# Two transformer layers on one core: the second layer's modulation made in the first feed-forward part, and the layer loop written out

## The chip, the core and the metric

The kernel runs on one core of a Trainium2 chip. The core has a matrix engine (TensorE, PE in the profile; PEld are its weight loads), VectorE (DVE), ScalarE (ACT), GpSimd (POOL) and SyncE (SP, here the main DMA queue). They run independently and wait for one another by semaphores. Weights and activations come from the chip's memory (HBM) by DMA into SBUF; PE writes its results to PSUM, eight banks of 512 fp32 columns. The metric is the device time of one execution in microseconds (us); lower is better.

## The reference, cut to what matters

Two layers run on 1024 latent tokens and 128 context tokens (1152 columns together), model width 1024. Each layer has its own modulation: a row of 6 x 1024 numbers from a conditioning vector, one for the context and one for the latents, which shifts, scales and gates both halves of the layer.

```python
for l in range(DEPTH):                                   # DEPTH = 2
    mod_ctx = silu(c_ctx) @ w_ada[l] + b_ada[l]          # w_ada[l]: 1024 x 6144
    mod_lat = silu(c) @ w_ada[l] + b_ada[l]
    ...
def trunk_layer(x, mod, ...):
    shift1, scale1, gate1, shift2, scale2, gate2 = split(mod, 6)
    h = rms_norm(x, g1) * (1 + scale1) + shift1
    x = x + gate1 * token_mixers(h, ...)                 # 6 MLA heads, 6 GQA heads, an FFT mixer, w_out
    h = rms_norm(x, g2) * (1 + scale2) + shift2
    x = x + gate2 * ((silu(h @ w_gate) * (h @ w_up)) @ w_down)   # width 2816
```

The modulation needs only the conditioning vectors and w_ada, so the kernel is free to place it anywhere ahead of its use.

## The kernel before

Everything lies transposed: channels on the 128 partitions, tokens in the columns, in three groups of 384. For precision each fp32 product is made of three matmuls on high and low parts (`mm3`, L1662 to L1666): GpSimd splits each weight unit of 128 x 1024 into w_hi (a cast, L851 and L918) and w_lo (a subtraction, L853 and L920), VectorE and ScalarE split the activations. All waits are written by hand, so the order on each engine is the order of the code.

The engines' programs are a preamble, a loop over the two layers (`Fori(0, DEPTH)`, a loop at run time on every engine; what depends on the layer is a register, and so are the values that its waits compare with), and the final norm. A layer is: norm, input projection, FFT mixer, up-projections; twelve heads, an MLA head and a GQA head in turn, in a function `pair` that runs for p = 0 to 5, the middle ones in a loop; the output projection w_out; the second norm; and the feed-forward part in 11 chunks of 256 hidden channels (a loop). One chunk is six tiles of gate and up (48 matmuls each) and 24 down units of 6 matmuls. VectorE's part of a tile is three operations (L1628 product, L1631 high part, L1633 low part); of a down unit, one or two (`add_gated`, L1606).

The modulation comes in 24 blocks of 512 columns, 12 per layer. Blocks 0 to 3 of layer 0 are made in the preamble by PE (`ada_w`). The others are made beside the heads, one block per head. SP loads the block, 2 MB in four DMAs, into `ada_buf` (`load_ada`, L720), which lies over the weight ring that the heads don't use. VectorE multiplies and adds it up over the eight rows of k, for context and latents (`ada_sums`, L1529, 16 operations of 512 columns, L1540 and L1542), three k ahead of the maxima of the next head, five behind. In the next head PE turns the sums from columns to partitions and adds over the partitions with 8 matmuls against ones (`ada_turn`, L1953, fp32, so 16 passes in the profile), and VectorE adds the bias into `mod` (`ada_add`, L1517, L1525). Which block head (p, w) makes is told by `late_chunk` (L246). In layer 0, heads 0 and 1 make blocks 0 and 1 of layer 1, heads 10 and 11 its blocks 2 and 3, the others layer 0's blocks 4 to 11. In layer 1 the same code makes layer 1's blocks 4 to 11, and heads 0, 1, 10 and 11 make layer 0's blocks 0 to 3 once more. The last head's block has its turn behind the heads (L1992).

Three things stand around this. GpSimd waits for all twelve blocks of the layer (L893) before it splits the first three units of w_out (L895), since the ring lies under `ada_buf` and `ada_acc`. Behind the heads, the heads' outputs come back from memory by `load_mix` (L754), one tile after another in a ring of four; each waits until `mix_low` (L1582, L1585) has made the low part of the tile four before it; PE's first out-projection tile needs eight of them. And SP loads the feed-forward weights (L794 to L804), each into one of three stages, as soon as GpSimd has split what was there.

In the heads PE makes the scores (L1899 to L1902), the products with V (L1917) and, for the next head, scores in full for the row maxima (`max_scores`, L1940), which VectorE reduces from PSUM (L1514); PE waits for each reduction before the next.

Of the kernel before, what the change touches and what calls it, by code (L numbers as in the profile page):

```python
# [245 lines left out]
def late_chunk(p, w, l):  # L246

    if isinstance(p, int) and p in (0, HEADS - 1):
        return l * -1 + 1, (0 if p == 0 else 2) + w
    return l, ADA_PRE + 2 * (p - 1) + w  # L250


def build(nc, a, o):
    ctx = ExitStack()
    with ctx:
# [48 lines left out]
        neg_max = keep("neg_max", [P, 16])  # L304
        y_stat = keep("y_stat", [P, 5, 9])
        ph = at[0]

        def phase(first, *tensors):
# [31 lines left out]
        qst_m, mq_hi, mq_lo, mk_hi, mk_lo, mv, ga, gb, ka, kb, gv, kst_g = phase(  # L340
# [3 lines left out]
            ("gv", [P, KT, P], F32), ("kst_g", [P, KEYS], F32))  # L344
# [8 lines left out]
        y_out, y_sq = phase(0, ("y_out", [P, 9, D_MODEL], F32), ("y_sq", [P, D_MODEL], F32))  # L353
# [72 lines left out]
        late_loaded = [sem(f"late_loaded{i}") for i in range(2)]  # L426
        late_mac, late_mm, late_ev = sem("late_mac"), sem("late_mm"), sem("late_ev")
# [85 lines left out]
        def _(sp):  # L513
# [29 lines left out]
            with sp.Fori(0, DEPTH) as l:  # L543
# [176 lines left out]
                def load_ada(p, w):  # L720

                    if p:
                        sp.wait_ge(late_mac, (l * NHEADS + 2 * (p - 1) + w + 1) * MACS)
                        settle(sp)
                    layer, q = late_chunk(p, w, l)
# [68 lines left out]
                with sp.Fori(0, CHUNKS) as c:  # L794
                    for j in range(6):
                        s = (U_FFN + j) % STAGES
                        sp.wait_ge(unit_split, l * UNITS + c * 6 + U_FFN + j + 1)
                        if j < 4:
                            src = (w_gate_v, w_up_v)[j % 2][l, c, j // 2]
                            dst = w_in_st[:, s, :].rearrange("p (k n) -> p k n", n=P)  # L800
                        else:
                            src = w_down_v[l, c, j - 4]
                            dst = w_in_st[:, s, :].rearrange("p (k n) -> p k n", n=512)
                        sp.dma_start(dst, src).then_inc(unit_loaded[s], 16)  # L804
# [15 lines left out]
        def _(pool):  # L820
# [5 lines left out]
            with pool.Fori(0, DEPTH) as l:  # L826
# [66 lines left out]
                pool.wait_ge(late_ev, (l + 1) * NHEADS)  # L893
# [32 lines left out]
        def _(act):  # L926
# [47 lines left out]
            with act.Fori(0, DEPTH) as l:  # L974
# [251 lines left out]
        def _(dve):  # L1226
# [85 lines left out]
            with dve.Fori(0, DEPTH) as l:  # L1312
# [8 lines left out]

                mod_l = mod[:, :, :].rearrange("p (l n) c -> p l n c", l=DEPTH)
# [194 lines left out]
                def ada_add(p, w, n):  # L1517

                    dve.wait_ge(late_mm, n + 1)
                    got = ps[:, 3, 0:16].rearrange("p (n c e) -> p n c e", c=2, e=2)[:, :, :, 0]  # L1520
                    dst = mod[:, :, :].rearrange("p (l q n) c -> p l q n c", l=DEPTH, n=4)
                    bias = b_ada_t[:, :].rearrange("p (l q n) -> p l q n", l=DEPTH, n=4)
                    layer, q = late_chunk(p, w, l)
# [3 lines left out]
                    ins.then_inc(late_ev, 1)  # L1527

                def ada_sums(p, w, k0, k1):  # L1529

                    y = l * NHEADS + 2 * p + w
                    if k0 == 0:
                        dve.wait_ge(late_loaded[w], (l * HEADS + p + 1) * 64)
                    for k in range(k0, k1):
                        if k:
                            dve.wait_ge(late_mac, y * MACS + 2 * k)
# [9 lines left out]
                def pair(p, first=False, last=False):  # L1546
                    for half in range(2):
# [4 lines left out]
                        if half or not first:  # L1552
                            ada_add(p - 1 + half, 1 - half, y - 1)
# [18 lines left out]
                pair(0, first=True)  # L1572
# [4 lines left out]
                ada_add(HEADS - 1, 1, l * NHEADS + NHEADS - 1)  # L1577
# [21 lines left out]
                dve.wait_ge(late_ev, (l + 1) * NHEADS)  # L1599
# [21 lines left out]
                nc.vector.memset(eps_t[:, 5:6], 0.0)  # L1621
                with dve.Fori(0, CHUNKS) as c:
                    for j in range(6):
# [37 lines left out]
        def _(pe):  # L1661
# [50 lines left out]
            with pe.Fori(0, DEPTH) as l:  # L1712
# [240 lines left out]
                def ada_turn(w, n):  # L1953

                    pe.wait_ge(late_mac, (n + 1) * MACS)
                    settle(pe)
                    for j in range(4):
                        for c in range(2):
                            at_col = 4 * j + 2 * c
                            ins = nc.tensor.matmul(ps[:, 3, at_col:at_col + 2], ada_acc[:, w, c, j * P:(j + 1) * P],  # L1960
                                                   ones[:, 0:2], start=True, stop=True)
                    ins.then_inc(late_mm, 1)

                def pair(p, first=False, last=False):
                    for half in range(2):
                        y = l * NHEADS + 2 * p + half
                        ada = half or not first
                        more = not (half and last)
                        for i in range(STEPS):
# [5 lines left out]
                            if ada and i == 1:  # L1975
                                ada_turn(1 - half, y - 1)
                            if more and MAX_AT <= i < MAX_AT + MAX_TILES:
                                max_scores(y + 1, 1 - half, i - MAX_AT, after_ada=y if ada else None)
# [9 lines left out]
                with pe.Fori(1, 5) as p:  # L1988
# [49 lines left out]
                with pe.Fori(0, CHUNKS) as c:  # L2038
# [114 lines left out]
```

## Time and profile before

| | us |
|---|---|
| median of 3 runs | 3691.17 |
| lowest, highest | 3688.93, 3691.19 |
| the profiled execution, its time | 3689.86 |
| its span, first to last instruction | 3688.0 |

The page divides the span into 40 slices of 92 us: PE is busy 8 to 9 tenths in nearly all, and the chain of waits lies on PE for 85% of the span, on VectorE for 8%, on DMAs for 2%. In time, the first layer's heads take from about 440 to 860 us, its feed-forward part from 1032 to 1861, the second layer's heads from about 2238 to 2658, its feed-forward part up to 3661. A row of the timeline gives the start, the duration and the engine; "[... <-X]" is how long the engine was idle before, and on what it waited. A row of the chain of waits is one link of the work that ended last, and says where the time of the kernel went. The granted clock is a share of PE's full 2.4 GHz; half of it is 1.2 GHz.

### The profile page before, as it was taken

Reading aid. Unit: us, or ns where it says so; the run is one execution under the profiler, and the core shown is the slowest. Engines: PE = TensorE matmul, PEld = TensorE weight load, DVE = VectorE, ACT = ScalarE, POOL = GpSimd, SP = SyncE. Lnnn points to the kernel's source line nnn. Section 1 sums busy time; section 2 is a strip of 40 time slices with the busy share of each in tenths; the row PEclk is TensorE's granted clock in tenths of the full one; section 3 lists DMA queues with packets and bytes.
Section 4 is the critical chain, followed back from the end, with each engine's and each line's share of the span. In section 5 each row is a group of like instructions: output and inputs, shape, how many; then the busy total and the mean of one; then the engine's idle time right before and its main releaser. Section 6 shows DMA issues by size and latency. Waiting matters only on the chain.

```text
span 3688.0 us, 49530 instructions
## 1 busy us (share of the span) xinstructions
PE 3449.7 (94%) x17888; PEld 2968.0 (80%) x17888; DVE 1737.5 (47%) x2758; ACT 735.7 (20%) x1334; POOL 789.6 (21%) x430
## 2 busy tenths in 40 slices
PE   7898899998989999999979988999988999999998
PEld 3887655556989999999969875555587999999998
DVE  1645566665163334333354366666534344333433
ACT  2322233333120000000032132333313000000001
POOL 1211111112222222222122101111121322222220
PEclk8997899998999999999989898999999999999999
DMA  5243633423111111111023335424120111111111
GB/s 186 73 146 105 178 96 114 119 77 88 43 35 45 43 36 45 45 34 45 23 59 118 118 125 149 122 84 125 51 87 29 52 45 34 45 45 34 45 34 51
DMA packets 297200, 279.70 MB, mean 76 GB/s; under 512 B 63922, under 2 KB 243908, under 8 KB 297076
## 3 DMA queue, kind: packets, MB, share of 16 engines
q1 hardware_dynamic: 268468, 242.74, 22.6%
q10 hardware_dynamic: 28608, 35.40, 2.6%
q8 instruction: 66, 1.08, 0.1%
q14 instruction: 58, 0.48, 0.0%
HBM read 230.20 MB, written 48.02 MB: 75 GB/s over the span
## 4 chain that ended last, share of the span: by engine, by line
PE 85%; DVE 8%; issue 2%; DMA 2%; ACT 1%; SPq 1%; POOL 0%; ACTq 0%; DVEq 0%; POOLq 0%
PE ps L1664 22%; PE ps L1666 22%; PE ps L1665 22%; PE ps L1917 9%; PE ps L1940 4%; DVE neg_max L1514 3%; PE ps L1705 2%; DVE h_lo L1299 1%; PE ps L1960 1%; PE ps L1726 1%; PE ps L1902 1%; PE ps L1901 1%; PE ps L1690 1%; PE ps L1949 1%; DVE wk L1289 1%
## 5 line engine op out<-in xcount | busy, mean ns | idle before, releaser
L1664 PE MATMUL ps<-h_hi,w_hi 128*128 128x384 f32 (+1 forms) x3072 | 1061.5, 346 | 79.8 <-DVE h_lo L1299 63.8
L1665 PE MATMUL ps<-h_lo,w_hi 128*128 128x384 f32 (+1 forms) x3072 | 1040.9, 339 | 0.0
L1666 PE MATMUL ps<-h_hi,w_lo 128*128 128x384 f32 (+1 forms) x3072 | 1040.2, 339 | 0.0
L1664 PEld LDWEIGHTS ps<-h_hi,w_hi 128*128 128x128 f32 (+1 forms) x3072 | 580.8, 189 | 95.3 <-issue 74.6
L1665 PEld LDWEIGHTS ps<-h_lo,w_hi 128*128 128x128 f32 (+1 forms) x3072 | 580.7, 189 | 11.3 <-issue 0.7
L1666 PEld LDWEIGHTS ps<-h_hi,w_lo 128*128 128x128 f32 (+1 forms) x3072 | 580.1, 189 | 3.2
L1606 DVE SCALAR_TENSOR_TENSOR x<-ps,lmod,x 128x384 f32<-128x384 f32 (+2 forms) x768 | 365.9, 512 | 317.7 <-PE ps L1666 317.6
L1628 DVE TENSOR_TENSOR wk<-ps,wk 128x384 f32<-128x384 f32 x132 | 73.6, 558 | 829.7 <-PE ps L1666 825.2
L1140 ACT ACTIVATE p_t<-ps 128x512 f32<-128x512 f32 (+1 forms) x456 | 264.7, 580 | 506.3 <-PE ps L1666 267.2
L1206 ACT ACTIVATE wk<-ps 128x384 f32<-128x384 f32 x132 | 64.7, 492 | 1468.5 <-PE ps L1666 1468.5
L1664 PE MATMUL ps<-act_hi,w_hi 128*128 128x384 f32 x1056 | 356.9, 338 | 0.0
L1666 PE MATMUL ps<-act_hi,w_lo 128*128 128x384 f32 x1056 | 355.9, 337 | 0.0
L1665 PE MATMUL ps<-act_lo,w_hi 128*128 128x384 f32 x1056 | 354.4, 336 | 0.0
L918 POOL CAST w_hi<-w_stage 128x1024 fp32r<-128x1024 f32 x120 | 125.4, 1045 | 1038.6 <-PE ps L1666 684.8
L1514 DVE TENSOR_REDUCE neg_max<-ps 128x1 f32<-128x1152 f32 (+1 forms) x216 | 266.8, 1239 | 168.3 <-PE ps L1940 158.2
L920 POOL TENSOR_TENSOR w_lo<-w_stage,w_hi 128x1024 fp32r<-128x1024 f32 x120 | 288.8, 2407 | 9.6
L851 POOL CAST w_hi<-w_stage 128x1024 fp32r<-128x1024 f32 (+2 forms) x64 | 68.8, 1075 | 884.9 <-PE ps L1666 312.7
L1542 DVE SCALAR_TENSOR_TENSOR ada_acc<-ada_buf,silu_c,ada_acc 128x512 f32<-128x512 f32 x336 | 242.5, 763 | 5.2
L1917 PE MATMUL ps<-p_t,gv 128*65 128x512 f32 (+1 forms) x456 | 225.6, 577 | 2.3 <-ACT p_t L1140 2.3
L1917 PE MATMUL ps<-p_t,mv 128*65 128x512 f32 (+1 forms) x456 | 227.7, 581 | 0.0
L1665 PEld LDWEIGHTS ps<-act_lo,w_hi 128*128 128x128 f32 x1056 | 198.3, 188 | 0.0
L1666 PEld LDWEIGHTS ps<-act_hi,w_lo 128*128 128x128 f32 x1056 | 198.2, 188 | 0.0
(249 smaller groups left out, 4140.8 us busy)
## 6 DMA issues: line engine op xcount, KB each, us to landing
ada_buf<-in_w_ada SPq DMA_DIRECT2D x96, 512.0 KB, 6.2
w_stage<-in_w_ffn_gate SPq DMA_DIRECT2D x44, 512.0 KB, 3.8
w_stage<-in_w_ffn_up SPq DMA_DIRECT2D x44, 512.0 KB, 3.8
w_stage<-in_w_ffn_down SPq DMA_DIRECT2D x44, 512.0 KB, 3.8
s_in<-ev_p ACTq DMA_DIRECT2D x66, 192.0 KB, 1.9
w_stage<-in_w_in SPq DMA_DIRECT2D x24, 512.0 KB, 3.9
ada_w<-in_w_ada SPq DMA_DIRECT2D x4, 2048.0 KB, 17.2
w_stage<-in_w_out SPq DMA_DIRECT2D x16, 512.0 KB, 4.9
```

What stands on the lines that cost most here:

```text
L918: pool.tensor_copy(w_hi[:, s, :], w_in_st[:, st, :]).then_inc(unit_hi, 1)
L920: pool.tensor_tensor(w_lo[:, s, :], w_in_st[:, st, :], w_hi[:, s, :].bitcast(F32), ALU.subtract).then_inc(unit_split, 1)
L1140: nc.scalar.activation(p_t[:, (half * STEPS + i) % 2, 0:w], s_bank(half, i)[:, 0:w], ACT.Exp)\
L1514: nc.vector.tensor_reduce(neg_max[:, t:t + 1], ps_flat[:, max_at:max_at + w], AX_X, ALU.max, negate=True).then_inc(max_done, 1)
L1542: ins = nc.vector.scalar_tensor_tensor(out=acc, in0=wt, scalar=s, in1=acc, op0=ALU.mult, op1=ALU.add)
L1606: ins = nc.vector.scalar_tensor_tensor(out=x[:, m, c0:c1], in0=ps[:, bank, c0 - g * GW:c1 - g * GW], scalar=lmod[:, gate + m, c:c + 1], in ...
L1664: nc.tensor.matmul(out, wh, xh, start=first, stop=False)
L1665: nc.tensor.matmul(out, wh, xl, start=False, stop=False)
L1666: return nc.tensor.matmul(out, wl, xh, start=False, stop=last)
L1705: nc.tensor.matmul(ps[:, 5 + g, 0:GW], ones[:, :], wk[:, i % 4, :], start=(k == 0), stop=(k == DK - 1)).then_inc(sq_used, 1)
L1917: nc.tensor.matmul(ps[0:VD + 1, GROUP_BANK[j], 0:w], (gv if half else mv)[:, kt, 0:VD + 1], p_t[:, (half * STEPS + i) % 2, 0:w], start=(i ...
L1940: ins = nc.tensor.matmul(ps_flat[:, max_at + c0:max_at + c0 + w], q[:, qs], k[:, CTX + c0:CTX + c0 + w], start=True, stop=True)
```

## The change

Every `Fori(0, DEPTH)` becomes a Python loop: each engine's program holds both layers one after the other, with constants in place of the layer register. Layer 0's heads now make nine blocks: layer 0's blocks 4 to 11 (heads 2 to 9) and block 11 of layer 1 (head 10); heads 0, 1 and 11 make none, and layer 1's heads none at all. Layer 1's blocks 0 to 10 are made in layer 0's feed-forward part, one per chunk, in 16 pieces of 256 columns and one k each: SP loads them into a ring of four (`f_buf`, 128 KB each), VectorE sums them behind the tiles (4, 3, 3, 3, 3 and 0 pieces), PE turns them ahead of down unit 4, VectorE adds the bias ahead of down unit 10. The guard of GpSimd's first w_out units falls from 12 blocks per layer to 9 in all. SP puts the block's loads between the third and the fourth weight load of the chunk after. `neg_max` and `y_stat` move to other places in SBUF.

```diff
-def late_chunk(p, w, l):
+LATE_HERE = 9
+F_TILES, F_RING, F_W = 16, 4, 256
+F_AFTER = ((0, 4), (4, 7), (7, 10), (10, 13), (13, 16), (16, 16))
+
+def late_chunk(p, w):
+    return (1, 11) if isinstance(p, int) and p == HEADS - 1 else (0, ADA_PRE + 2 * (p - 1) + w)
+
+def has_late(l, p, w):
+    return l == 0 and not (isinstance(p, int) and (p < 1 or p >= HEADS or p == HEADS - 1 and w == 1))
...
+        f_acc, f_buf = phase((2 * DK + 2) * T * 4, ("f_acc", [P, 2, 512], F32), ("f_buf", [P, F_RING, F_W], F32))
...
-            with sp.Fori(0, DEPTH) as l:
+            for l in range(DEPTH):
...
+                def load_next_ada(q, first=False):
+                    for n in range(F_TILES):
+                        if n >= F_RING or not first:
+                            sp.wait_ge(f_mac, (q * F_TILES + n - F_RING + 1) * 2)
+                            settle(sp)
+                        half, k = divmod(n, DK)
+                        sp.dma_start(f_buf[:, n % F_RING, :], w_ada_v[1, q][:, k, F_W * half:F_W * half + F_W])\
+                            .then_inc(f_loaded[n % F_RING], 16)
+
+                if l == 0:
                     for j in range(6):
...
+                        load_ffn(0, j)
+                    for j in range(3):
+                        load_ffn(1, j)
+                    load_next_ada(0, first=True)
+                    for j in range(3, 6):
+                        load_ffn(1, j)
+                    with sp.Fori(2, CHUNKS) as c:
+                        for j in range(3):
+                            load_ffn(c, j)
+                        load_next_ada(c - 1)
+                        for j in range(3, 6):
+                            load_ffn(c, j)
+                    load_next_ada(CHUNKS - 1)
...
-                pool.wait_ge(late_ev, (l + 1) * NHEADS)
+                pool.wait_ge(late_ev, LATE_HERE)
...
+                if l:
+                    dve.wait_ge(f_ev, CHUNKS)
...
+                def next_ada(q, n):
+
+                    half, k = divmod(n, DK)
+                    at_ = slice(F_W * half, F_W * half + F_W)
+                    dve.wait_ge(f_loaded[n % F_RING], (q * (F_TILES // F_RING) + n // F_RING + 1) * 16)
+                    if k:
+                        dve.wait_ge(f_mac, (q * F_TILES + n) * 2)
+                    for c in range(2):
+                        acc, wt, s = f_acc[:, c, at_], f_buf[:, n % F_RING, :], silu_c[:, c, k:k + 1]
+                        if k == 0:
+                            ins = nc.vector.tensor_scalar(acc, wt, s, None, ALU.mult)
+                        else:
+                            ins = nc.vector.scalar_tensor_tensor(out=acc, in0=wt, scalar=s, in1=acc, op0=ALU.mult,
+                                                                 op1=ALU.add)
+                        ins.then_inc(f_mac, 1)
...
+                        for i in range(*F_AFTER[j] if l == 0 else (0,)):
+                            next_ada(c, i)
                     for d in range(G * DK):
+                        if l == 0 and d == 10:
+                            dve.wait_ge(f_mm, c + 1)
+                            mod_add(1, c, 7).then_inc(f_ev, 1)
...
-                pe.wait_ge(late_ev, (l + 1) * NHEADS - 1)
-                ada_turn(1, l * NHEADS + NHEADS - 1)
...
+                        if l == 0 and d == 4:
+                            pe.wait_ge(f_mac, (c + 1) * F_TILES * 2)
+                            turn(f_acc, 7).then_inc(f_mm, 1)
```

`turn` is the body of `ada_turn`, and `mod_add` that of `ada_add`, for any sums and any bank.

## Rows read from the trace of the kernel before

**Rows 1.** busy time of the whole span (page, part 1: busy us, share, instructions)

```profile
PE 3449.7 (94%) x17888; PEld 2968.0 (80%) x17888; DVE 1737.5 (47%) x2758; ACT 735.7 (20%) x1334; POOL 789.6 (21%) x430
```

**Rows 2.** the span in 100 us windows: PE, PEld, DVE, ACT, POOL busy us, clock, DMA

```profile
1200.00:1300.00 100.00, 100.00 (x578) 100.00 (x577) 35.71 (x59) 5.71 (x10) 27.52 (x16) 1.00 0.14 42
2300.00:2400.00 100.00, 98.69 (x385) 56.41 (x384) 66.91 (x84) 38.50 (x66) 17.80 (x6) 1.00 0.38 112
2680.00:2686.00 6.00, 6.00 (x20) 6.00 (x21) 3.54 (x3) 0.52 (x1) 3.16 (x2) 0.54 0.66 185
```

**Rows 3.** the chain of waits inside an odd head: start us, us, what

```profile
2421.48 1.68 PE ps L1960 x16
2423.16 0.91 PE ps L1917 x2
...
2425.86 0.86 PE ps L1917 x2
...
2427.74 1.37 DVE neg_max L1514
```

**Rows 4.** line L1960, all its matmuls, and who waited for them

```profile
L1960 PE MATMUL ps<-ones,ada_acc x384: 165/251/251, 479.2 to 2660.0; 128*128 128x2 f32 x192
...
  DVE mod L1525: 133.6, 24
```

**Rows 5.** end of the second layer's heads, timeline, cut to some rows

```profile
2658.38 1.85 PE L1960 MATMUL ps<-ones,ada_acc 128*128 128x2 f32 x16
...
2661.05 1.04 POOL L851 CAST w_hi<-w_stage 128x1024 fp32r<-128x1024 f32 x1 [58.25 <-DVE mod L1525]
...
2666.18 2.35 POOL L853 TENSOR_TENSOR w_lo<-w_stage,w_hi 128x1024 fp32r<-128x1024 f32 x1
...
2667.11 1.84 DVE L1585 TENSOR_TENSOR h_lo<-wk,h_hi 128x384 fp32r<-128x384 f32 x1
...
2670.64 2.24 DVE L1585 TENSOR_TENSOR h_lo<-wk,h_hi 128x384 fp32r<-128x384 f32 x1
...
2673.27 0.55 DVE L1585 TENSOR_TENSOR h_lo<-wk,h_hi 128x384 fp32r<-128x384 f32 x1
```

**Rows 6.** VectorE's lines L1542 and L1628 (count: ns min/median/max)

```profile
L1542 DVE SCALAR_TENSOR_TENSOR ada_acc<-ada_buf,silu_c,ada_acc x336: 740/747/3277, 438.8 to 2648.5; 128x512 f32<-128x512 f32 x168
...
L1628 DVE TENSOR_TENSOR wk<-ps,wk x132: 544/558/559, 1052.2 to 3635.8; 128x384 f32<-128x384 f32 x132
```

**Rows 7.** the first feed-forward chunk and a later one, timeline of the SP queue, VectorE

```profile
1057.78 0.37 SPq L804 DMA_DIRECT2D w_stage<-in_w_ffn_gate  x1
...
1055.27 0.55 DVE L1628 TENSOR_TENSOR wk<-ps,wk 128x384 f32<-128x384 f32 x1
...
1113.23 0.37 SPq L804 DMA_DIRECT2D w_stage<-in_w_ffn_gate  x1
...
1117.81 0.56 DVE L1628 TENSOR_TENSOR wk<-ps,wk 128x384 f32<-128x384 f32 x1 [7.77 <-PE ps L1666]
```

**Rows 8.** the same stretch, the chain of waits

```profile
2674.06 4.78 DMA wk<-s_fnet
```

**Rows 9.** a feed-forward tile that meets GpSimd: timeline of VectorE and GpSimd

```profile
1361.07 2.65 DVE L1633 TENSOR_TENSOR act_lo<-wk,act_hi 128x384 fp32r<-128x384 f32 x1
...
1360.90 2.40 POOL L920 TENSOR_TENSOR w_lo<-w_stage,w_hi 128x1024 fp32r<-128x1024 f32 x1
```

**Rows 10.** from the first layer's last addition to the second layer's start, chain of waits

```profile
1861.14 2.82 issue
...
1865.16 2.23 DVE lvec L1327
...
1868.65 0.53 ACT wk L957
```

**Rows 11.** ScalarE's evictions ahead of the second heads, chain of waits

```profile
2199.34 0.45 ACT ev_q L1027
...
2200.30 0.45 ACT ev_q L1027
```

More of the change, by code:

```diff
@@ L243, with late_n @@
 MACS = 2 * DK
-def late_chunk(p, w, l):
-    if isinstance(p, int) and p in (0, HEADS - 1):
-        return l * -1 + 1, (0 if p == 0 else 2) + w
-    return l, ADA_PRE + 2 * (p - 1) + w
+LATE_HERE = 9
[5 more added lines that the diff above has]
+    return l == 0 and not (isinstance(p, int) and (p < 1 or p >= HEADS or p == HEADS - 1 and w == 1))
+def late_n(p, w):
+    return 2 * (p - 1) + w
 def build(nc, a, o):
@@ L426, in build @@
         late_loaded = [sem(f"late_loaded{i}") for i in range(2)]
+        f_loaded = [sem(f"f_loaded{i}") for i in range(F_RING)]
+        f_mac, f_mm, f_ev = sem("f_mac"), sem("f_mm"), sem("f_ev")
         late_mac, late_mm, late_ev = sem("late_mac"), sem("late_mm"), sem("late_ev")
@@ new lines, in _ @@
+                if l == 0:
+                    for j in range(6):
+                        load_ffn(0, j)
[11 more added lines that the diff above has]
+                    load_next_ada(CHUNKS - 1)
+                else:
+                    with sp.Fori(0, CHUNKS) as c:
+                        for j in range(6):
+                            load_ffn(c, j)
@@ L972, in norm_x @@
                         root_x(g + 1)
-            with act.Fori(0, DEPTH) as l:
+            for l in range(DEPTH):
                 act.wait_ge(lay_ready, l + 1)
@@ L1310, in norm_split @@
                     low(i)
-            with dve.Fori(0, DEPTH) as l:
+            for l in range(DEPTH):
                 steps = [0]
@@ L1544, in ada_sums, with pair @@
                             ins.then_inc(late_mac, 1)
-                def pair(p, first=False, last=False):
+                def pair(p, last=False):
                     for half in range(2):
@@ L1551, in pair @@
                             highs(y + 1, p + half, half == 1)
-                        if half or not first:
-                            ada_add(p - 1 + half, 1 - half, y - 1)
+                        ada_add(p - 1 + half, 1 - half)
                         ada_sums(p, half, 0, 3)
@@ L1571, in _ @@
                     max_tile(l * NHEADS, t, first=True)
-                pair(0, first=True)
+                pair(0)
                 pair(1)
@@ L1710, in sum_squares @@
                     sum_square(n0, i, *divmod(i, DK))
-            with pe.Fori(0, DEPTH) as l:
+            for l in range(DEPTH):
                 def unit(u, n):
@@ L1966, in pair @@
                         y = l * NHEADS + 2 * p + half
-                        ada = half or not first
+                        before = (p - 1 + half, 1 - half)
+                        ada = has_late(l, *before)
                         more = not (half and last)
@@ L1975, in pair @@
                             if ada and i == 1:
-                                ada_turn(1 - half, y - 1)
+                                ada_turn(*before)
                             if more and MAX_AT <= i < MAX_AT + MAX_TILES:
-                                max_scores(y + 1, 1 - half, i - MAX_AT, after_ada=y if ada else None)
+                                max_scores(y + 1, 1 - half, i - MAX_AT, after_ada=late_n(*before) + 1 if ada else None)
                             if more and i == ROW_AT:
```

75 lines of the change are left out of this document (41 added, 34 removed).

## The prediction

> **What bounds the kernel now.** I read the page's busy times first: PE is busy 3449.7 of 3688.0 us and VectorE 1737.5 [rows 1]. A share of the whole span says nothing about one stage, so the windows come next [rows 2]. In the feed-forward part PE is busy 100.00 of 100 us at full clock, with VectorE at 35.71: whatever PE is given there lengthens the kernel one for one, and VectorE has room. In the heads PE is busy 98.69 and VectorE 66.91: again PE is nearly alone. The chain of waits inside a head says how nearly: it runs over PE's products and steps onto VectorE only for the row maxima, 1.37 us each [rows 3]; the sums of the modulation (L1542) never stand in it. So the VectorE work that moves is off the path at its old place; what is on the path is PE's turning of each finished block (L1960). The third reading is of the seams, where PE waits: the end of each layer's heads and the step from layer 0 to layer 1.
>
> **PE's turns.** One block costs PE 16 passes: 1.68 us, and the product behind them takes 0.91 instead of 0.86 [rows 3], so 1.73 us. VectorE waited for such turns 24 times [rows 4], 12 in each layer's heads, of which the twelfth stands behind the last head, where PE has nothing else to do [rows 5]: 22 are on the path. After, layer 0 keeps 9 (all inside the heads), layer 1 none. Heads: 22 - 9 = 13 fewer, -13 x 1.73 = -22.5 us. The feed-forward part of layer 0 gets one turn per chunk, 11, each in a stream with no gap [rows 2]: +11 x 1.73 = +19.0 us. 24 blocks become 20, since the second layer's heads had recomputed four blocks of layer 0 that nothing reads. Net -3.5 us. No row shows a turn among 384-column matmuls: I bound it by 1.5 and 2.2 us, since the 16 passes are the same and only the edges differ, which is +16.5 to +24 for the eleven.
>
> **VectorE's sums in the feed-forward part.** Per chunk 16 pieces of 256 columns, two operations each. At 512 columns one takes 0.747 us [rows 6]; L1542 has 336 of them. 256 columns cost between 0.37 us (the straight line through L1628's 384 columns in 0.558 [rows 6] and this one) and 0.56 (as much as 384); I take 0.45, so 32 x 0.45 = 14.4 us per chunk (12 to 18). A chunk is 432 matmuls at 578 per 100 us [rows 2], 75 us, and a tile 48 of them, 8.3 us; VectorE goes from 36% to about 55%. Up to four pieces follow one tile's products, 3.6 us; the tile's own three operations take some 1.5, and VectorE was idle 7.77 us ahead of a tile [rows 7]. PE needs a tile's product only three tiles later (L2059), and the down part needs the last acts, behind which no piece stands (the sixth entry of F_AFTER is empty). So nothing is late: 0 us in steady state. The two additions per block (L1525's kind) wait for a turn that PE did six tiles earlier: nothing. Behind that wait on VectorE stand the down additions; PE holds six banks.
>
> The first chunk is tighter. VectorE comes out of the norm late, its second tile is at 1055.27, and SP issues the third weight load of the next chunk at 1057.78 [rows 7]; the first pieces are issued behind it and land some 3 us later. VectorE now waits there with tiles 1 to 5 queued behind; adding four, three, three, three, three pieces brings the last tile's acts to about 1089, where PE wants them (the down part's sixth unit) at about 1090. I take +1 us, bounds 0 and 6. In the next chunk that weight load is issued at 1113.23 and the first product is at 1117.81 [rows 7], its acts end 1.5 later: the pieces, issued by 1115, are there in time.
>
> **Queues passed.** SP now waits for VectorE's sums between the third and the fourth weight load of a chunk. The fourth goes out when 12 pieces are done, behind the fourth tile, about 37 us into the chunk instead of 25 (three tiles); GpSimd splits it at about 50 us, when the sixth tile ends. 13 us of room: nothing. The heads lose the loads of 15 blocks of 24; no step of the chain there is a load.
>
> **GpSimd's first three splits of w_out.** They waited for the last block's addition (58.25 us idle, released by L1525) and so fell into the seam, 2661 to 2672 [rows 5]. There the chain runs over VectorE's h_lo (L1585), which takes 0.55 us alone but 1.84 and 2.24 while GpSimd's subtraction runs [rows 5]: 1.29 + 1.69 = 3.0 us. With the guard at 9 the splits fall into the last head (layer 0) or the one before it (layer 1). There VectorE has only reductions from PSUM; a PSUM-fed line like L1628 never exceeded 0.559 us in 132 executions [rows 6] though GpSimd was busy 27% of the time. Behind the h_lo is a load of 4.78 us [rows 8], which starts that much earlier but follows other loads and PE's rows, so I take 2.8 of 3.0 per layer: -5.6 us, bounds -9 (PE's first 6 us ran at a granted 0.54, the 1.2 GHz level [rows 2], and may be spared a part) and 0.
>
> Here a rule speaks against the change. The rows show L1633 at 2.65 us as it meets GpSimd's subtraction of 2.40 [rows 9], and L1542 at up to 3.277 [rows 6]. The Trainium skill (SBUF — State Buffer, SBUF: two separate sides) says that a VectorE instruction with two SBUF inputs and a GpSimd one that reads SBUF exclude each other for a whole instruction. By that rule all new sums can be held up, and can hold up the splits; if every one of six subtractions hits a piece, that is 6 x 2.4 = 14.4 us more per chunk on VectorE, 40 + 14 in 75, still without a wait of PE's. That is the rival below.
>
> **The layers written out.** At the step to layer 1 VectorE stands still for 2.82 us with nothing to wait for, then its copies meet GpSimd (L1327, 2.23 us), and ScalarE's squares, on which PE waits, start at 1868.65 [rows 10]. The jump back over the whole layer is the only thing there, and it goes. Some register steps between the copies go too; the collision partly stays: -3.3 us, bounds 0 and -5. The Trainium skill (Runtime: NRT & Kernel Launch, Instruction fetch mechanics) says that a taken branch to a target outside the fetched window stalls for the fetch. By that rule the 2.82 go for good; the row agrees.
>
> Waits on constants need no register step. Where ScalarE evicts ahead of the heads its period is 0.96 us, of which 0.45 is the copy [rows 11]; about 0.15 of it may go, and then PE limits at six matmuls of 320 columns, 6 x 0.173 x 320 / 384 = 0.87 us (100 us / 578 [rows 2]): 12 x 0.1 in each layer. With small steps elsewhere I take -2 us, bounds 0 and -8.
>
> **Sum.** -22.5 + 19.0 + 1 - 5.6 - 3.3 - 2 = -13.4. The profiled execution took 3689.86 us (span 3688.0), so 3676.5; the median of the runs, 3691.17, is 1.3 higher, so I forecast 3677.5.
>
> **Rivals.** (1) PE waits for VectorE in layer 0's feed-forward part. It decides when a tile's acts, its pieces and the GpSimd subtractions they meet exceed 8.3 us two tiles in a row. If a piece's operation kept the 0.747 us of the full width, 24 us of pieces, 9 of acts and up to 20 of collisions would stand in 50 us of tiles, some 3 us too much; 11 x 3 = 33, and the time is 3677.5 + 33 = 3710. For it: L1542's 3.277; against it: half the columns and 7.77 us idle ahead of a tile. Chance 7%, slower. (2) The seams don't move: the load of 4.78 us and PE's rows end last after all, and the next layer's code has to be fetched with or without a jump. Then only -3.5 + 1 and -1 from constants remain: 3691.2 - 3.5 = 3687.7. Chance 13%, within 0.2%. For it: the load stands in the chain [rows 8]. (3) More goes: PE's idle time at the seams gets short enough that less of it runs at 1.2 GHz, and register steps counted in many short chains: -9 - 5 - 8 - 3.5 = -25.5, 3665.7. Chance 12%. (4) That the change doesn't do what it says can be left out: the diff issues 11 turns and drops 15. The forecast itself, 3672 to 3683: 68%.
>
> **How the numbers follow.** A measurement of this kernel can tell about 0.2%, 7.4 us. Faster by more: forecast and (3), 80%. Within: (2), 13%. Slower: (1), 7%. The range leaves out (1) and half of (3)'s tail: 3666 to 3689.
>
> **What would show it.** Right: L1960's kind 20 times, none in layer 1's heads; each head there shorter by 1.7 us; layer 0's chunks 76.8 us instead of 75.1; GpSimd's w_out splits ahead of the last head's end; L1585 at 0.55 in the seam; no 2.8 us gap of VectorE's at the step to layer 1. Wrong: chunks above 78 us or PE waiting for act_done or down_add (rival 1); the seam's DMA issued no earlier (rival 2).

## The result, and where the time went

The changed kernel took 3670.27 us (median of 7 runs, 3664.36 to 3685.82) beside 3691.17 (7 runs, 3688.93 to 3697.31) of the kernel before on the same chip: ratio 0.9951, 95% interval 0.9932 to 0.9969. On a second chip it took 3670.1 beside 3692.5 (0.9939, 0.9926 to 0.9952). The forecast was 3677.5, with a range of 3666 to 3689.

The first profiled execution is the slowest of its seven, 3685.82 us with a span of 3683.6, only 4.4 us under before's 3688.0. Judged by it alone the change would have brought almost nothing. So a second profile, of the same kernel on the second chip, stands beside it (span 3664.8), and each stage is read in both. Stages are cut at fixed instructions of the program: the end of a head's last row maximum (VectorE's L1562, before L1514), the last product with V, the point where a norm's gains are ready, VectorE's product for the first tile of a chunk. "Act" below is such a product; "the reciprocal" is VectorE's L1632 (before L1580), the first step behind the heads. Stretches that the table leaves out (the preamble, the second norm up to the first act, the end) moved by 1.5 us at most each.

| us | before | after, first profile | after, second |
|---|---|---|---|
| ahead of the heads, layer 0; layer 1 | 347.3; 350.8 | 348.3; 349.6 | 343.8; 347.5 |
| heads 1 to 11 and the last products, layer 0 | 425.6 | 421.9 | 420.4 |
| the same, layer 1 | 425.5 | 405.0 | 404.8 |
| last product to second norm, layer 0; 1 | 53.7; 54.6 | 48.4; 49.0 | 49.9; 47.7 |
| first feed-forward chunk, layer 0 | 65.6 | 68.5 | 70.2 |
| the next nine chunks, layer 0 | 675.8 | 692.8 | 692.0 |
| last chunk and step to layer 1 | 74.1 | 72.4 | 72.4 |
| feed-forward part of layer 1 | 807.1 | **817.6** | 807.9 |

All rows but the last move the way that the forecast has them, some by more, with one exception of 1 us (ahead of layer 0's heads, first profile). The last row is 10.5 us in a stage whose work the change leaves as it was, and the second profile doesn't show it.

The page's busy times, which answer [rows 1]:

```profile
PE 3453.5 (94%) x17824; PEld 2975.6 (81%) x17824; DVE 1712.7 (46%) x2862; ACT 734.8 (20%) x1334; POOL 785.5 (21%) x430
```

64 matmul records fewer: four blocks of 16. The windows of the first profile, for [rows 2] (PE, PEld, DVE, ACT, POOL busy us with counts, clock, DMA share, GB/s):

```profile
1200.00:1300.00 100.00, 100.00 (x583) 100.00 (x583) 56.55 (x111) 5.71 (x10) 27.51 (x16) 1.00 0.22 65
2300.00:2400.00 100.00, 98.37 (x353) 53.51 (x352) 36.71 (x33) 40.74 (x70) 17.88 (x6) 1.00 0.22 51
2666.25:2672.25 6.00, 6.00 (x26) 5.75 (x28) 3.44 (x3) 0.52 (x1) 3.42 (x3) 0.72 0.66 186
3200.00:3300.00 100.00, 100.00 (x569) 100.00 (x568) 32.02 (x57) 5.71 (x10) 26.73 (x16) 1.00 0.14 42
```

VectorE in the feed-forward part went from 35.71 to 56.55 us of 100, in layer 1's heads from 66.91 to 36.71, the way that was forecast. The third line is six us from the out-projection's first matmul on; it comes back under "Seams". The last line is layer 1's feed-forward part: PE is 100% busy at full clock, and yet does 569 matmuls in 100 us. The same window of the second profile:

```profile
3200.00:3300.00 100.00, 100.00 (x578) 100.00 (x577) 35.71 (x59) 5.71 (x10) 27.52 (x16) 1.00 0.14 42
```

578, as in the kernel before [rows 2]. Between starts, the 384-column matmuls of gate and up stood 173.3 ns apart in one execution and 176.7 in the other (alternately 174 and 179), for the whole layer; 288 of them a chunk, 3.4 ns each, make up the 0.96 us by which its chunks are longer (76.05 against 75.09). The time from one start to the next is called the cadence below.

The added work, grouped by line (count: ns min/median/max, first and last start; then who waited for it):

```profile
L1686 DVE SCALAR_TENSOR_TENSOR f_acc<-f_buf,silu_c,f_acc x308: 471/480/2628, 1058.2 to 1844.0; 128x256 f32<-128x256 f32 x154
L2032 PE MATMUL ps<-ones,f_acc x176: 165/251/251, 1082.7 to 1854.2; 128*128 128x2 f32 x176
...
  PE ps L2032: 1.1, 1
```

A piece's operation takes 0.48 us (the forecast took 0.45), at most 2.63. PE waited once for the sums, 1.1 us, in the first chunk; from the second to the last chunk of layer 0 it waited for nothing.

The seam behind layer 1's heads, for [rows 5] (timeline, cut to some rows):

```profile
2595.11 1.03 POOL L897 CAST w_hi<-w_stage 128x1024 fp32r<-128x1024 f32 x1
...
2600.87 1.36 DVE L1562 TENSOR_REDUCE neg_max<-ps 128x1 f32<-128x1152 f32 x1 [0.88 <-PE ps L2013]
...
2653.50 0.95 DVE L1632 RECIPROCAL sums<-sums 108x128 f32<-108x128 f32 x1 [37.11 <-DMA sums<-s_sum]
...
2654.60 7.91 PE L2080 MATMUL ps<-sums,ident 108*64 108x128 f32 x84 [6.25 <-DVE sums L1632]
...
2656.72 0.55 DVE L1637 TENSOR_TENSOR h_lo<-wk,h_hi 128x384 fp32r<-128x384 f32 x1
...
2658.00 0.55 DVE L1637 TENSOR_TENSOR h_lo<-wk,h_hi 128x384 fp32r<-128x384 f32 x1
...
2664.66 1.04 POOL L897 CAST w_hi<-w_stage 128x1024 fp32r<-128x1024 f32 x1 [59.18 <-DMA w_stage<-in_w_out]
...
2664.98 3.77 DVE L1637 TENSOR_TENSOR h_lo<-wk,h_hi 128x384 fp32r<-128x384 f32 x2 [1.67 <-DMA wk<-s_fnet]
...
2666.25 0.41 PE L1737 MATMUL ps<-h_hi,w_hi 128*128 128x384 f32 x1 [3.74 <-DVE h_lo L1637]
```

GpSimd's first three splits of w_out now lie in the heads, where VectorE's maxima beside them keep their length (1.36, before 1.37 [rows 3]). In the seam VectorE's h_lo takes 0.55 for the tiles that those splits used to meet, PE's rows run in one piece of 84, and the out-projection starts 12.7 us after the reciprocal (before: 16.2). One collision stays, with GpSimd's fourth split: the two h_lo behind the load of s_fnet take 1.1 and 2.7 us, as in the kernel before (1.0 and 2.7), and the first of them is the last thing that PE waits for. The step to layer 1, for [rows 10]:

```profile
1875.53 0.62 DVE L1658 SCALAR_TENSOR_TENSOR x<-ps,lmod,x 128x384 f32<-128x384 f32 x1 [0.43 <-PE ps L1739]
1876.18 0.54 DVE L1371 COPY lmod<-mod 128x32 f32<-128x32 f32 x1
...
1876.85 2.31 DVE L1375 COPY lvec<-vecs 128x8 f32<-128x8 f32 x1
...
1880.33 1.76 ACT L1003 ACTIVATE wk<-x 128x384 f32<-128x384 f32 x4 [35.44 <-DVE gs L1385]
```

The copy follows the last addition at once, and the one copy of 2.31 us (2.23 in [rows 10]'s chain) beside GpSimd's subtraction stayed. Finally ScalarE's evictions ahead of the heads, for [rows 11]:

```profile
2215.49 0.44 ACT L1073 ACTIVATE ev_q<-ps 128x320 f32<-128x320 f32 x1 [0.46 <-PE ps L1739]
...
2216.38 0.44 ACT L1073 ACTIVATE ev_q<-ps 128x320 f32<-128x320 f32 x1 [0.46 <-PE ps L1739]
```

Their period is 0.89 us instead of 0.96, and they now wait for PE: six of its matmuls take 0.88.

### The profile page after: what moved, and what is told of

Its sections match the earlier page's. It is cut to its first block and busy times, and to the rows that moved or that the text cites. A ratio compares the mean times of both kernels' runs of the same rounds, so it can differ in the third digit from the quotient of the medians.

```text
span 3683.6 us, 47585 instructions
## 1 busy us (share of the span) xinstructions
PE 3453.5 (94%) x17824; PEld 2975.6 (81%) x17824; DVE 1712.7 (46%) x2862; ACT 734.8 (20%) x1334; POOL 785.5 (21%) x430
## 5 line engine op out<-in xcount | busy, mean ns | idle before, releaser
L1562 DVE TENSOR_REDUCE neg_max<-ps 128x1 f32<-128x1152 f32 (+1 forms) x216 | 266.8, 1239 | 275.5 <-PE ps L2013 266.1
L1737 PEld LDWEIGHTS ps<-act_hi,w_hi 128*128 128x128 f32 x1056 | 197.8, 187 | 0.0
```

Source lines behind the costliest of these rows:

```text
L1562: nc.vector.tensor_reduce(neg_max[:, t:t + 1], ps_flat[:, max_at:max_at + w], AX_X, ALU.max, negate=True).then_inc(max_done, 1)
L1737: nc.tensor.matmul(out, wh, xh, start=first, stop=False)
```

## The experiments

They ran in three groups, each on a chip of its own beside the kernel before (3692.46, 3693.18 and 3692.51 us), so between groups differences of 1 or 2 us of medians mean nothing. Each group's kernel before is the one that a ratio is taken against. "Turn" is PE's 16 passes, "sums" are VectorE's pieces.

**The changed kernel again.** No edit.

> The changed kernel once more, unedited. In its first profile the gate and up matmuls of the whole feed-forward part of layer 1 started every 176.7 ns instead of 173.3 ns (76.05 us per chunk instead of 75.09, 10.6 us for eleven chunks). Theory A: this is a property of one execution (two phases that the stream of matmuls can lock into), so this profile may show 75.1 us per chunk and a span near 3671; the unprofiled times spread over more than 10 us. Theory B: it belongs to this program (its addresses or its code), so the profile shows 76.05 us per chunk again. Time: 3664 to 3682 under either.

Measured: 3670.1 us (3666.93 to 3671.36), layer 1's chunks at 75.09. The slower cadence does not belong to the program, which rules theory B out. This profile is from another chip than the first, so by itself it can't tell an execution from a chip. The times of single chips speak for the execution: the seven of the first chip spread from 3664.36 to 3685.82, and those of turns only, further down, fall into two pairs 10 us apart.

**The layers written out, nothing else.**

```diff
-            with dve.Fori(0, DEPTH) as l:
+            for l in range(DEPTH):
```
(the same on the other four engines)

> The kernel before with its two layers written out on all five engines and nothing else. By the prediction's terms: the step to layer 1 -3.3 us, constants -2 us, so 3686 us, with no 2.8 us gap of VectorE at the step. Rival: the code of the next layer has to be fetched with or without a jump, and the time stays within 1 us of 3691. Of the change's roughly 18 us this run gives the part that the writing out alone brings.

Measured: 3681.38 us, ratio 0.9967 (0.9955 to 0.998). That is -11.1 us, twice the forecast's -5.3 and half of the whole gain. The step to layer 1 gave the expected part: 74.06 to 70.64. The rest lies in amounts of up to 3 us ahead of the heads, in them, and in layer 1's seam, of a size by which stages also differ between executions.

**Written out on all engines but PE.** The same edit on four engines; PE keeps this line:

```diff
             with pe.Fori(0, DEPTH) as l:
```

> The kernel before with the layers written out on SyncE, GpSimd, ScalarE and VectorE, while PE keeps its loop over the layers. Writing out on all five gave -11 us where the prediction had -5.3. Theory A: the excess is in PE's own register steps between short matmuls ahead of the heads and in the seams; then this kernel stays 4 to 7 us above the one written out everywhere, 3686 to 3688. Theory B: it is in ScalarE's and VectorE's evictions and chains; then it is at 3681 to 3683.

Measured: 3680.78 us, ratio 0.997 (0.9959 to 0.9981): PE's own register steps are worth nothing that this can tell, so theory A is out. Theory B's time came, though nothing here shows that ScalarE and VectorE carry it.

**VectorE alone, ScalarE alone written out.** From the kernel before, one engine's line each.

```diff
-            with act.Fori(0, DEPTH) as l:
+            for l in range(DEPTH):
```

> The kernel before with only VectorE's layers written out (SyncE, GpSimd, ScalarE and PE keep their loop). All five written out gave -11.1 us, all but PE -12.4. Theory: the gain is VectorE's, its jump back of 2.8 us and its register steps in short chains ahead of the heads and in the seams: -8 to -12 us, so 3681 to 3685. Rival: ScalarE's jump (2.5 us) and its evictions ahead of the heads carry most: then 0 to -4 us, 3689 to 3693.

> The kernel before with only ScalarE's layers written out. Theory: most of the gain is VectorE's, so 0 to -4 us: 3689 to 3693. Rival: ScalarE's evictions ahead of the heads (two sets of twelve at a period of 0.96 us, and its copies in the seams) carry it: -6 to -10 us, 3683 to 3687.

Measured: 3688.17 us (ratio 0.9992, 0.9981 to 1.0004) and 3688.29 (0.9987, 0.9977 to 0.9997). Each gives some 4 us by the medians, 3 to 5 by the ratios, with intervals that reach to nothing or nearly; neither carries the gain alone, so VectorE's theory (-8 to -12) and ScalarE's rival (-6 to -10) are both out. SyncE and GpSimd were not written out alone. The traces settle one part of it. VectorE alone, then ScalarE alone, at the step to layer 1:

```profile
1864.31 0.62 DVE L1606 SCALAR_TENSOR_TENSOR x<-ps,lmod,x 128x384 f32<-128x384 f32 x1 [0.43 <-PE ps L1666]
1864.96 0.55 DVE L1323 COPY lmod<-mod 128x32 f32<-128x32 f32 x1
```

```profile
1863.22 0.62 DVE L1606 SCALAR_TENSOR_TENSOR x<-ps,lmod,x 128x384 f32<-128x384 f32 x1 [0.43 <-PE ps L1666]
1866.95 0.88 DVE L1323 COPY lmod<-mod 128x32 f32 x1 [3.10 <-issue]
```

The 3.4 us at the step go with VectorE's loop, and its idle time of 3.10 us with them. The Trainium skill (Runtime: NRT & Kernel Launch, Instruction fetch mechanics) says that a taken branch to a target outside the fetched window stalls until the target is fetched. The trace agrees in that the gap stands where the jump is and goes with it; that the engine was fetching, no row shows. ScalarE's part is its evictions: their period falls from 0.977 us to 0.897 (medians) only where ScalarE is written out. That is 0.08 x 12, 1 us per layer. The remaining 6 us or so of the 11 (11.1 - 3.4 - 2) are not traced to a place; stages vary by 1 to 3 us between executions, and one profile of each can't tell more.

**GpSimd's splits back into the seam.**

```diff
-                pool.wait_ge(late_ev, LATE_HERE)
+                pool.wait_ge(pv_mm, (l + 1) * NHEADS * STEPS)
```

> The changed kernel with one wait put later: GpSimd's first splits of w_out wait for the last product of the last head again, instead of the ninth block. Theory: the seams from the reciprocal to the second norm go back from 43.3 and 43.8 us to 48.4 and 49.3, +10.5 us in all over the changed kernel, and VectorE's h_lo subtractions there last about 2 us instead of 0.55. Rival: the seams got shorter because the last turn and addition behind the heads are gone and PE came to the out-projection at a higher clock; then less than 3 us come back.

Measured: 3672.64 us (3668.74 to 3684.13), ratio 0.9955 (0.9941 to 0.9969): 2.5 us above the changed kernel, not 10.5, as the rival had it. But the trace shows that the edit undid only half:

```profile
2646.11 1.04 POOL L897 CAST w_hi<-w_stage 128x1024 fp32r<-128x1024 f32 x1 [53.46 <-PE ps L1990]
...
2651.01 0.95 DVE L1632 RECIPROCAL sums<-sums 108x128 f32<-108x128 f32 x1 [37.14 <-DMA sums<-s_sum]
```

GpSimd starts 4.9 us ahead of the reciprocal; in the kernel before it waited for the last block's turn and addition and started 2.8 us ahead of it. Of its three subtractions one was over before the reciprocal, and the second ran until 2.0 us after it, ahead of the first tile's h_lo at 3.2; in the kernel before two of the three ran beside VectorE's h_lo, here one did. So the edit was made stronger:

```diff
-                pool.wait_ge(late_ev, LATE_HERE)
+                pool.wait_ge(rec_done, l + 1)
```

> The changed kernel with GpSimd's first splits of w_out released by the reciprocal, 3.8 us later than in the kernel before (the run with them at the last product began 1.9 us earlier than the kernel before, and gave back only 2.5 us of the 10.5 expected). Theory: the splits now lie fully beside VectorE's h_lo, so the first out-projection matmul is 2.5 to 3 us later after the reciprocal than the 12.9 and 12.7 us of the changed kernel, in both layers: +5 to +6 us, 3675 to 3676. Rival: VectorE's chain has room there, PE's first matmul moves by less than 1 us, and the time stays at 3670 to 3672.

Measured: 3675.82 us (3670.3 to 3677.72), ratio 0.9948 (0.9935 to 0.996): +5.7 us over the changed kernel by the medians, +3 by the ratios. Its time alone wouldn't decide; the trace does, and it agrees with the theory. Layer 1's seam in its timeline:

```profile
2654.43 2.36 POOL L899 TENSOR_TENSOR w_lo<-w_stage,w_hi 128x1024 fp32r<-128x1024 f32 x1
...
2655.29 1.91 DVE L1637 TENSOR_TENSOR h_lo<-wk,h_hi 128x384 fp32r<-128x384 f32 x1
...
2658.89 2.24 DVE L1637 TENSOR_TENSOR h_lo<-wk,h_hi 128x384 fp32r<-128x384 f32 x1
...
2662.83 2.24 DVE L1637 TENSOR_TENSOR h_lo<-wk,h_hi 128x384 fp32r<-128x384 f32 x1
...
2667.53 0.66 PE L1737 MATMUL ps<-h_hi,w_hi 128*128 128x384 f32 x1 [3.02 <-DVE h_lo L1637]
```

From the reciprocal to the out-projection's first matmul, layers 0 and 1, us: 15.4 and 15.5 here; 15.4 and 15.6 with only the layers written out; 14.2 and 13.8 with the half undoing; 13.0 and 12.7 in the changed kernel's second profile (12.6 to 13.0 in its two profiles and in those of its three cut versions further down). The splits' place is worth some 2.6 us per layer (15.4 and 15.5 less 13.0 and 12.7).

**No feed-forward part of the modulation; turns only; sums only.** The first has all three edits below, turns only the first two (PE then waits for no sums), sums only the third. What layer 1 needs of the modulation is left out.

```diff
-                    for n in range(F_TILES):                          (no loads)
+                    for n in ():
-                        for i in range(*F_AFTER[j] if l == 0 else (0,)):   (no sums)
+                        for i in ():
-                        if l == 0 and d == 4:                         (no turns)
+                        if False:
```

> The changed kernel without the eleven blocks in layer 0's feed-forward part: no loads, sums, turns or additions there; layer 1's modulation of blocks 0 to 10 is left out and set to zero. Theory: -19.8 us (11 turns at 1.80) and -1.2 us (first chunk), so 21 us below the changed kernel, with layer 0's chunks at 75.1 us. Rival: VectorE's sums disturb PE's stream, or the slower cadence of 176.7 ns in layer 1's chunks comes from the turns' work; then 25 to 32 us.

Measured: 3648.42 us (ratio 0.9875, 0.986 to 0.9889), 21.7 below the changed kernel, chunks of layer 0 at 75.09, as the theory had it.

> The changed kernel with PE's eleven turns in layer 0's feed-forward part, but none of VectorE's sums and none of their loads (the turned block is zero, so layer 1's modulation of blocks 0 to 10 is left out). It splits the 21.7 us that the whole feed-forward part of the modulation costs (3670.1 against 3648.4 without it). Theory: it is all PE's, so chunks take 76.9 us as with the sums, and the time is 3648.4 + 19.8 = 3668; only the 1 to 5 us of the first chunk are missing. Rival: part of the 1.80 us per chunk is PE being held up by VectorE's sums, and a chunk is nearer 75.09 + 1.68 = 76.77 or less.

Measured: 3674.36 us, four runs in two pairs: 3667.32 and 3670.48, 3678.24 and 3680.76. The profiled one (3678.24) is of the upper pair, with layer 1's chunks at 76.05. The lower pair is the theory's time of 3668, the upper one adds the slower cadence. Layer 0's chunks take 76.89, with the sums and without, so the rival is out; the turn's own 16 passes take 1.70 of the 1.80 us.

> The changed kernel with VectorE's sums and their loads, but no turn of PE's and no additions (layer 1's modulation of blocks 0 to 10 is left out). Theory: chunks of layer 0 take 75.09 us again although VectorE is busy some 20 us more in each, except the first, which keeps its wait for the first pieces: 65.25 + 1 to 5 us. Time 3648.4 + 1 to 5 = 3650 to 3653. Rival: the sums slow PE's stream or its evictions, and chunks are above 75.2 us.

Measured: 3650.14 us (3649.8 to 3652.53), chunks of layer 0 at 75.09, the first 66.94 instead of 65.25. The windows 1400 to 1500 us, turns only, then sums only:

```profile
1400.00:1500.00 100.00, 100.00 (x583) 100.00 (x582) 37.69 (x67) 4.72 (x8) 27.54 (x16) 1.00 0.14 42
```

```profile
1400.00:1500.00 100.00, 100.00 (x578) 100.00 (x577) 53.04 (x107) 5.71 (x10) 27.45 (x17) 1.00 0.25 75
```

With the sums VectorE is at 53.04 and DMA at 0.25, and PE does its 578 matmuls all the same. So 19.8 of the 21.7 us are PE's turns (11 x 1.80), and what the sums cost, 1.7 us, lies in the first chunk.

**A version meant to be faster: rows instead of turns.** VectorE splits each finished half block into two parts, high and low, and PE streams these past a stationary operand that is 1 in one column and 0 elsewhere, so that each row lands in its own place of one PSUM bank; four transposes at the end of the layer turn all 22 rows.

```diff
+                    for c in range(2):
+                        for src in (f_hi, f_lo):
+                            nc.tensor.matmul(ps[0:FR, 7, F_W * half:F_W * half + F_W],
+                                             f_z[:, 3 - c:3 - c + FR], src[:, c, :], start=False, stop=False)
```

> A version meant to be faster: the block is not turned by 16 passes with the block as the stationary operand; VectorE splits each finished half block into a high and a low F32R part, and PE streams these (4 matmuls of 256 columns per half, one-hot stationary operand of 22 columns) into one PSUM bank that collects all 22 rows; four transposes at the end of layer 0 turn them all. By the rows: eight matmuls of 256 columns at one column per cycle of 2.4 GHz are 0.85 us per chunk instead of 1.80, so -0.9 x 11 = -10 us, +1.5 us at the step to layer 1 for the copy and the transposes, so 8 us below the changed kernel: 3662. Rival: the short matmuls don't stream at full rate (each costs its weight load besides, 0.15 us or more), and the time is 3668 to 3672.

Measured: 3703.96 us (ratio 1.0028, 1.0018 to 1.0038), outside both expectations. What PE waited for in the first chunks is most of it:

```profile
PE ps L2166 <- DVE f_z L1691: 34.8, 1, 34.8
PE ps L1775 <- DVE x L1671: 4.2, 3, 1.4
```

The clearing of the bank stood ahead of the first chunk and waited for VectorE to come out of the norm. Most of the 34.8 us is a wait that PE has there anyway; what it added is 8.9 us (from the second norm to the first act 148.6 us instead of 139.7 in the changed kernel's second profile). And the last pieces stood ahead of the down additions: 1.4 us per chunk. The passes themselves cost 0.92 us per chunk instead of 1.70.

For the mended version no piece stands behind a chunk's last tile, and the clearing moves to the first chunk's passes (PE's first and last chunk are written out for it):

```diff
-F_AFTER = ((0, 3), (3, 6), (6, 8), (8, 11), (11, 14), (14, 16))
+F_AFTER = ((0, 3), (3, 6), (6, 8), (8, 12), (12, 16), (16, 16))
-                if l == 0:
-                    pe.wait_ge(f_ev, 1)
-                    nc.tensor.matmul(ps[0:FR, 7, 0:512], f_z[:, 22:44], h_hi[:, 0, 0:512], start=True, stop=False)
+                    if opening:
+                        nc.tensor.matmul(ps[0:FR, 7, 0:512], f_z[:, 22:44], h_hi[:, 0, 0:512], start=True, stop=False)
```

> The version with rows, with its two waits of PE taken out: no pieces behind the last tile of a chunk (in its first profile PE stood 1.4 us per chunk ahead of the down part), and the bank's clearing inside the first chunk instead of ahead of it (9 us). The last chunk's part is written out so that the transposes lie beside the down additions. In its first profile the eight matmuls cost 0.92 us per chunk against 1.70 for the turn. By that chunks of 76.0 us, -0.78 x 11 = -8.6 us, +0.9 us for the transposes: 3662. Rival: the resumptions left the stream of matmuls in its slower cadence (176.7 ns) in parts of each chunk, and that stays: up to 3.4 ns x 432 = 1.5 us per chunk, 3662 + 16 = 3678.

Measured: 3678.24 us (3673.72 to 3685.45), ratio 0.9956 (0.9943 to 0.9968). That is the rival's value, but by luck: the cadence took 0.66 us per chunk, 7 us in all, instead of the rival's 16, and the rest is a wait that neither foresaw, in the first chunk:

```profile
PE ps L2159 <- DVE f_lo L1716: 7.5, 1, 7.5
```

And the chunks take 76.67 us where 76.01 were expected. Starts in a gate and up stream around four of the passes:

```profile
1295.18 0.34 PE L1777 MATMUL ps<-h_lo,w_hi 128*128 128x384 f32 x1
1295.35 0.34 PE L1778 MATMUL ps<-h_hi,w_lo 128*128 128x384 f32 x1
1295.53 0.34 PE L1776 MATMUL ps<-h_hi,w_hi 128*128 128x384 f32 x1
1295.70 0.34 PE L1777 MATMUL ps<-h_lo,w_hi 128*128 128x384 f32 x1
1295.88 0.34 PE L1778 MATMUL ps<-h_hi,w_lo 128*128 128x384 f32 x1
1296.06 0.28 PE L2162 MATMUL ps<-f_hi,f_z 128*22 128x256 f32 x1
...
1296.52 0.34 PE L1776 MATMUL ps<-h_hi,w_hi 128*128 128x384 f32 x1
1296.69 0.34 PE L1777 MATMUL ps<-h_lo,w_hi 128*128 128x384 f32 x1
1296.87 0.34 PE L1778 MATMUL ps<-h_hi,w_lo 128*128 128x384 f32 x1
1297.04 0.34 PE L1776 MATMUL ps<-h_hi,w_hi 128*128 128x384 f32 x1
1297.21 0.34 PE L1777 MATMUL ps<-h_lo,w_hi 128*128 128x384 f32 x1
```

Five steps ahead of the passes are 0.88 us, 176 to 177 ns each. Behind them four are 0.69, 173 ns. This repeats: the next gate and up stream, behind the passes in the down part, is at 176.7 again (58 matmuls in 1354 to 1364 us), and the passes in the midst of each end it (60 in 1298 to 1308). So the cadence has two settled values, and here it moves from one to the other at what is put into the stream. The version is no gain: the 0.78 us saved per chunk are spent on the cadence and on the 7.5 us.

## Why the forecast was right, point by point

**Heads.** -22.5 for 13 turns. Measured in the first profile -3.7 in layer 0 (2 turns) and -20.5 in layer 1 (11 turns), -24.2 in all, and -25.9 in the second; 1.1 of it comes with writing out alone. The count was right, and the price nearly: 1.86 us per turn in layer 1, where 1.73 was taken.

**Turns in the feed-forward part.** +19.0; measured 1.80 us per chunk, +19.8. The sums only and turns only kernels show that it is PE's time and nothing of VectorE's: the forecast's "0 us in steady state" holds, and rival (1) is out. VectorE's operations of up to 2.63 us had room. The Trainium skill (SBUF — State Buffer, SBUF: two separate sides) says that a VectorE instruction with two SBUF inputs and a GpSimd one that reads SBUF hold each other up for whole instructions. The trace agrees: VectorE's h_lo of 0.55 became 1.91 and 2.24 with the splits beside it.

**First chunk.** +1 (0 to 6). By the sums only it is +1.7. In the changed kernel it was 68.5 and 70.2 us against 65.6, less the turn's 1.8: +1.1 and +2.8. In the second of them PE had waited 0.9 us for the last sum and then, behind the turn, ran 10 matmuls 320 ns apart, at the lower clock (granted 0.72 in 1078 to 1084 us). In the first it had waited 1.1 us and stayed at full clock (granted 1.00 over the turn and behind it), so the wait by itself doesn't decide that. The mechanism was the one described, its size at the near end.

**Seams.** -5.6 for the splits. Their place is worth some 2.6 us per layer, so the step was right. Yet the stage from the last product to the second norm fell by 5.3 and 5.6 in one profile, by 3.8 and 6.9 in the other. Some of the excess comes with writing out (layer 1's stage from the reciprocal to the norm was 46.4 us there instead of 49.3). Some lies behind the first matmul. In layer 1 the granted clock of the first 6 us there is 0.72 in both profiles, against 0.54 before [rows 2]. But it doesn't go with the splits' place: in layer 0 the changed kernel has 0.72 in one profile and 0.55 in the other, the layers written out alone have 0.68 in layer 1 with the splits still in the seam, and the splits at the reciprocal 0.76 in layer 0. A high or a low value comes and goes between executions, and what decides it stays open.

**Step to layer 1.** -3.3; measured -3.4, by VectorE's jump.

**Constants instead of registers.** -2 (0 to -8). This is the step that was mis-sized: writing out gave -11.1, so some -7.7 beside the step to layer 1, where -2 was taken. The one place that was worked out, ScalarE's evictions, was right (0.08 us each, 0.1 forecast), and PE limits there now. About 6 us more have no place found. That they are register steps in many short chains, as rival (3) has it, is likely but not shown.

**The sum.** -13.4 was forecast. (The terms give 3677.8; the forecast's 3677.5 is a slip of rounding.) In medians -20.9 was measured on the first chip and -22.4 on the second, of which -11.1 by writing out (forecast -5.3) and -11.3 by the moved modulation and splits (forecast -8.1). For the second part the stages above give only 7 to 8 us: 23 to 25 off the heads and 5 off the seams, 20 for the turns and 1 to 3 for the first chunk on top. So about 4 us of it are not placed either. The result lies in the range, but 1.7 us below the band 3672 to 3683 that got 68%, and nearer to rival (3)'s 3665.7 than to the forecast. That the forecast way held is due to its mechanisms; that the time stayed in the range, with the constants at four times their price, is owed to the width of the range. By the first profile alone (-4.4 us) the forecast gain would have seemed three times too large; by the medians it was too small by 7 to 9 us.

## What to carry to other kernels

Where one engine is full in one stage and another has room in it, price a move by the full engine's instructions first: here 15 us of VectorE's time per chunk cost nothing from the second chunk on and 1.7 us in the first, where VectorE came late, and PE's 16 passes cost 1.8 us per chunk. The turns taken out of the heads and put into the feed-forward part nearly cancel; half of the gain is the written-out loop. So try the writing out of a loop over a few large bodies as its own change before anything is read from a larger one. And an experiment that undoes a wait must be looked at in the trace: putting the splits "back" to a nearly equal event undid half and seemed to refute what was true.

## What the chip showed that was not expected

In the gate and up part a stream of 384-column F32R matmuls, each with its own 128-column stationary operand, runs at full clock at 173.3 or at 176.7 ns from start to start. The down part's matmuls stand 174.8 ns apart on the average in either case. In layer 1 the value stays the same through eleven chunks. In layer 0 of the changed kernel's first profile it was seen to change twice: the first chunk ran at 173.3, the second, behind PE's wait of 1.1 us, at 176.7, and from the third on, behind the second turn, it was 173.3 again. Two windows, in the second and the third chunk:

```profile
1110.00:1150.00 40.00, 40.00 (x228) 40.00 (x227) 20.58 (x42) 2.41 (x5) 6.88 (x4) 1.00 0.30 92
1190.00:1230.00 40.00, 40.00 (x233) 40.00 (x232) 22.86 (x47) 2.64 (x6) 7.44 (x5) 1.00 0.27 82
```

The later turns, one per chunk, left the 173.3 as it was. In layer 1's feed-forward part the slower value was there in 4 of 14 profiled executions (the changed kernel's first, turns only, both versions with rows), for the whole layer, and it costs 10.4 us, 0.28%. All four are of the seven with something of the modulation on PE in layer 0's feed-forward part; the seven without it had none. That it hangs on this isn't shown: single runs of kernels without it lie just as far above their fellows (all but PE written out: six runs at 3677 to 3682, one at 3691.04). What sets the cadence when the stream starts stays open, and no experiment tried to set it in layer 1.
